# One stage for the first norm, the row projection and the query projection of a hybrid attention layer

## The reference

```
h = rmsnorm(x, norm1_g)                # x: 1024 prompt rows and 32 sample rows, 1024 wide
z = h @ w_in                           # 2848 columns
q_fox, k_fox, v_fox = 512 columns each       # 8 forgetting-attention heads of 64
f     = 8 columns -> logf = log_sigmoid(f + b_forget), later summed along the sequence
q_nsa = 512 columns                          # 8 sparse-attention heads
nsa   = 512 columns, win = 256 columns       # keys and values of the sparse attention and its window
gates = 24 columns -> sigmoid
```

## Time and profile before

| | |
|---|---|
| median of 3 runs | 2229.72 us (2228.98 to 2230.72) |
| profiled execution, its own time | 2237.79 us |
| span of the profiled execution | 2236.1 us |
| PE busy | 1909.3 us, 85% |
| DVE, ACT, POOL busy | 997.5, 723.5, 555.0 us |
| mean granted PE clock | 0.916 of full |

### The profile page before, as it was taken

The page is one execution under the profiler, slowest core; times in us unless marked ns, Lnnn a source line. Parts: engine busy times, 40 slices in busy tenths (PEclk is TensorE's granted clock), DMA queues, the critical chain, the costliest instruction groups (busy, mean ns, idle before and its releaser), DMA issues. The chain is left out here.

```text
span 2236.1 us, 32314 instructions
## 1 busy us (share of the span) xinstructions
PE 1909.3 (85%) x11816; PEld 1676.1 (75%) x11816; DVE 997.5 (45%) x1872; ACT 723.5 (32%) x1433; POOL 555.0 (25%) x644
## 2 busy tenths in 40 slices
PE   3996897996574738999999969899999999979996
PEld 2886796775552438788888858699999999966674
DVE  2323323112231324677777755433323333356897
ACT  2223112111221201777777753211211121133352
POOL 4310012124515132122222130111212222143452
PEclk9897898998786855999999989999999999989998
DMA  5532536322958283222222032211111111054533
GB/s 136 96 77 87 179 131 232 113 93 68 304 173 266 91 157 73 60 63 58 66 57 58 1 125 85 66 52 43 47 47 40 54 38 56 28 190 150 179 132 130
DMA packets 175169, 229.18 MB, mean 102 GB/s; under 512 B 44140, under 2 KB 120357, under 8 KB 174919
## 3 DMA queue, kind: packets, MB, share of 16 engines
q1 hardware_dynamic: 147930, 146.09, 21.8%
q0 software_dynamic: 27120, 81.55, 12.9%
HBM read 192.62 MB, written 40.18 MB: 104 GB/s over the span
## 5 line engine op out<-in xcount | busy, mean ns | idle before, releaser
L2290 DVE TENSOR_TENSOR pa_probs_T_lo<-pa_t,pa_probs_T_hi 128x512 fp32r<-128x512 f32 (+3 forms) x288 | 147.6, 533 | 64.5 <-ACT pa_probs_T_hi L2231 63.6
L121 PE MATMUL gate_acc<-o_T_hi,w_gate_split_hi 128*128 128x352 f32 x528 | 171.6, 325 | 2.0 <-ACTq L2669 2.0
L121 PE MATMUL up_acc<-o_T_hi,w_up_split_hi 128*128 128x352 f32 x528 | 170.4, 323 | 0.7 <-DVEq L2712 0.7
L122 PE MATMUL gate_acc<-o_T_lo,w_gate_split_hi 128*128 128x352 f32 x528 | 170.3, 323 | 0.0
L123 PE MATMUL gate_acc<-o_T_hi,w_gate_split_lo 128*128 128x352 f32 x528 | 170.2, 322 | 0.0
L122 PE MATMUL up_acc<-o_T_lo,w_up_split_hi 128*128 128x352 f32 x528 | 169.2, 321 | 0.0
L123 PE MATMUL up_acc<-o_T_hi,w_up_split_lo 128*128 128x352 f32 x528 | 169.1, 320 | 0.0
L2231 ACT ACTIVATE pa_probs_T_hi<-pa_t 128x512 fp32r<-128x512 f32 (+3 forms) x288 | 131.8, 472 | 91.3 <-PE pa_t L2156 88.0
L2156 PE MATMUL pa_t<-ident,pa_scores 128*128 128x128 f32 x816 | 138.9, 276 | 17.6 <-DVE pa_probs_T_lo L2290 17.6
L2216 ACT ACTIVATE pa_scores<-pa_scores,pa_neg_max 128x128 f32<-128x128 f32 (+1 forms) x192 | 143.3, 746 | 30.3 <-DVE pa_neg_max L2254 26.0
L121 PE MATMUL y_acc<-w_down_split_hi,act_split_hi 128*128 128x512 f32 x308 | 125.3, 407 | 18.9 <-DVE act_split_lo L3034 18.9
(11 more groups left out here) (444 smaller groups left out, 4773.5 us busy)
## 6 DMA issues: line engine op xcount, KB each, us to landing
w_down_raw<-in_w_down SPq DMA_DIRECT2D x59, 512.0 KB, 4.7
fox_k_pages<-in_cache_fox_kv SPq DMA_DIRECT2D x64, 256.0 KB, 8.3
w_rows<-in_cache_fox_kv POOLq DMA_DIRECT2D x64, 256.0 KB, 6.5
w_gate<-in_w_gu SPq DMA_DIRECT2D x22, 512.0 KB
w_up<-in_w_gu SPq DMA_DIRECT2D x22, 512.0 KB
sel_pages<-in_cache_nsa_kv POOLq DMA_DIRECT2D x64, 128.0 KB, 7.5
pa_k_fox<-scratch_kf_d POOLq DMA_DIRECT2D x32, 256.0 KB
w_rows<-in_w_in SPq DMA_DIRECT2D x3, 2048.0 KB, 14.5
```

The costliest lines, as they stand in the source:

```text
L121: pe.matmul(out, a[0][at], b[0][bt], start=start, stop=False)
L122: pe.matmul(out, a[0][at], b[1][bt], start=False, stop=False)
L2290: dve.tensor_tensor(lo, PT[n % 2][:, 0:m * P].rearrange("p (m n) -> p m n", n=P), hi, ALU.subtract).then_inc(s_cd, 1)
```

## The change

The three stages norm, queries and rows become one, `project`. Its steps are the 36 steps of the row stage, and behind them 24 query steps (chunks 4 and 5, q_fox and q_nsa with 512 columns each; twelve steps per chunk, 128 columns by a third of the rows). They use the same `z_acc`, `z` and `kt` buffers and the same weight buffers as the row steps.

- **Norm.** The tiles 0 and 1 are normalised and turned ahead of the first product. Tile t + 2 is normalised and turned around step t of the first chunk (k_fox): the steps need only their own tile of `hT`.
- **Loads.** The opening issues the loads of the first two tiles of `x` (once its tables are made) and of the k_fox weights (once its last page rows are turned). For this the weight buffers `w_rows`, the tiles of the norm and the second split weight buffer have fixed places at the far end of SBUF (`far_end`), and the opening's page rows and raw weights lie there too.
- **Log forget and gates.** The chain is spread over the query steps: ACT in steps 2 to 5 of the queries, DVE in 5, 6, 9 and 10, PE in 7, POOL's stores after 9 and 13. The sums are now kept in rows 64 to 71 of `c.cum`, which are zeroed again at the end.
- **Query results.** 128 x 352 per step: ACT copies with the scale, DVE splits into `kt`, POOL stores the pieces.

The core of the diff:

```diff
@@ front, SP @@
             load_rows(sp, mybir.EngineType.SP, 2, 0)
+            sp.wait_ge(s_pe, 4)
+            for t in range(2):
+                sp.dma_start(c.n1_x[t][:, :], d["x_prompt"][0, t * P:(t + 1) * P, :]).then_inc(c.s_x1[t], 16)
+            sp.wait_ge(s_tr, len(turns))
+            sp.dma_start(c.wr[0][:, :, :], d["w_in"][0].rearrange("(k p) n -> p k n", p=P)[:, :, C_KF:C_KF + 512]).then_inc(c.s_wr[0], 16)
...
+def project(c):
...
+    steps = [(ci, t) for ci in range(4) for t in range(NR)] + [(ci, x) for ci in (4, 5) for x in range(12)]
...
+            sp.dma_start(g[:, :], d["norm1_g"][0:1, :].to_broadcast([P, D])).then_inc(s_g, 16)
+            for t in range(2, 4):
+                sp.dma_start(x[t][:, :], d["x_prompt"][0, t * P:(t + 1) * P, :]).then_inc(c.s_x1[t], 16)
+            sp.dma_start(w[1][:, :, :], w_in[:, :, C_VF:C_VF + 512]).then_inc(s_w[1], 16)
+            for t in range(4, NR):
+                sp.wait_ge(s_xn, t - 3)
...
+            def product(s):
+                ci, t = steps[s]
                 if s >= 2:
                     pe.wait_ge(s_z, s - 1)
+                if ci == 0:
+                    pe.wait_ge(s_nl, t + 1)
...
+            turn_x(0)
+            turn_x(1)
+            n = 0
+            for s, (ci, t) in enumerate(steps):
+                product(s)
+                if ci == 0 and t + 2 < NR:
+                    turn_x(t + 2)
                 if n < len(tsteps) and tsteps[n] < s:
                     transposes(n)
                     n += 1
...
+            squares(0)
+            root(0)
+            rounded(0, [0])
+            squares(1)
+            root(1)
+            rounded(0, [1])
+            copy(0)
+            rounded(0, [2, 3])
+            copy(1)
+            for s, (ci, t) in enumerate(steps):
+                if ci == 0 and t + 2 < NR:
+                    squares(t + 2)
+                    root(t + 2)
+                if ci and t == 1 and ci + 1 < len(chunks):
+                    rounded(ci + 1, range(PIECES))
+                evacuated(s)
+                if ci == 0 and t + 2 < NR:
+                    copy(t + 2)
+                if ci == 0 and t + 2 == NR - 1:
+                    rounded(1, range(PIECES))
...
+            scale(0)
+            rests(0, [0])
+            scale(1)
+            rests(0, [1])
+            rest(0)
+            rests(0, [2, 3])
+            rest(1)
...
             for s, (ci, t) in enumerate(steps):
+                if ci == 0 and t + 2 < NR:
+                    scale(t + 2)
+                if n < len(ksteps) and ksteps[n] < s:
+                    key_copies(n)
+                    n += 1
+                if ci == 0 and t + 2 < NR:
+                    rest(t + 2)
+                if ci == 0 and t + 2 == NR - 1:
+                    rests(1, range(PIECES))
```

More of the change, by code:

```diff
@@ L276, in front @@
         w1 = split(ph, "cmp_w1_split", [P, 2, 16, 256])
-        raw = [ph.sb(f"cmp_w1_raw{i}", [P, 8, 256]) for i in range(2)]
+        rows = [ph.far(f"cmp_rows{i}", [P, 4, 4, 2, HD]) for i in range(SB)]
+        raw = [ph.far(f"cmp_w1_raw{i}", [P, 8, 256]) for i in range(2)]
         w2 = c.w2
@@ L808, in project_rows @@
     }
-    steps = [(ci, t) for ci in range(4) for t in range(9)]
+    steps = [(ci, t) for ci in range(4) for t in range(NR)] + [(ci, x) for ci in (4, 5) for x in range(12)]
+    rowwise = [ci < 4 for ci, t in steps]
+    NROW = sum(rowwise)
+    FIRST_Q = NROW
     KP = 2
@@ L839, in project_rows @@
         tp = [ph.ps(f"z_tp{i}", [P, 4, P]) for i in range(2)]
-        lp = [ph.ps(f"lf_tp{i}", [P, 4, P]) for i in range(3)]
+        ntp = [ph.ps(f"n1_tp{i}", [P, KD, P]) for i in range(2)]
+        lp = [ntp[0][:, 0:4, :], ntp[0][:, 4:8, :], ntp[1][:, 0:4, :]]
+        s_g = ph.sem("n1_gain_loaded")
+        s_ss, s_ms, s_rt, s_rr, s_xn = (ph.sem(f"n1_{n}") for n in ("squares", "mean", "root", "inverse", "normed"))
+        s_nt, s_nh, s_nl = (ph.sem(f"n1_{n}") for n in ("turned", "copied", "rest_kept"))
         s_hi = ph.sem("w_rows_rounded")
@@ L880, in _, with turn_x @@
         def _(pe):
+            def turn_x(t):
+                rows = ROWS[t]
+                pe.wait_ge(s_xn, t + 1)
+                if t >= 2:
+                    pe.wait_ge(s_nl, t - 1)
+                for k in range(KD):
+                    ins = pe.transpose(ntp[t % 2][:, k, 0:rows], xn[t % 2][0:rows, k * P:(k + 1) * P], c.ident[0:rows, 0:rows])
+                ins.then_inc(s_nt, 1)
             def transposes(n):
@@ L930, in _, with evacuated @@
-            rounded(0)
-            for s, (ci, t) in enumerate(steps):
-                rows = ROWS[t]
-                if t == 1 and ci + 1 < len(chunks):
-                    rounded(ci + 1)
+                    act.wait_ge(s_acc, sum(1 for a, t in steps if a < ci - 1))
+                for k in pieces:
+                    at = np.s_[:, k * KP:(k + 1) * KP, 0:width(ci)]
+                    act.activation(ws[ci % 2][0][at], w[ci % 2][at], ACT.Copy).then_inc(s_hi, 1)
+            def evacuated(s):
+                ci, t = steps[s]
@@ L954, in stores_before, with scale @@
         def stores_before(n):
[L955 removed]
+            return sum(1 for m in range(n) if m % 2 == n % 2 and kept(m))
         @block.vector
         def _(dve):
+            def scale(t):
+                rows = ROWS[t]
+                dve.wait_ge(s_ss, t + 1)
+                dve.tensor_scalar(ms[0:rows, t:t + 1], ss[0:rows, t:t + 1], 1.0 / D, EPS, ALU.mult, ALU.add).then_inc(s_ms, 1)
+                dve.wait_ge(s_rt, t + 1)
+                dve.reciprocal(rr[0:rows, t:t + 1], rt[0:rows, t:t + 1]).then_inc(s_rr, 1)
+                dve.wait_ge(s_rr, t + 1)
+                if t == 0:
+                    dve.wait_ge(s_g, 16)
+                if t >= 2:
+                    dve.wait_ge(s_nt, t - 1)
+                dve.scalar_tensor_tensor(out=xn[t % 2][0:rows, :], in0=x[t % 4][0:rows, :], scalar=rr[0:rows, t:t + 1],
+                                         in1=g[0:rows, :], op0=ALU.mult, op1=ALU.mult).then_inc(s_xn, 1)
@@ L1074, in _ @@
-            pool.wait_ge(s_fo, 48)
+                pool.wait_ge(s_ks[i], 32 * sum(1 for m in range(len(ksteps)) if m % 2 == i and kept(m)))
+            pool.wait_ge(s_fo, 32)
 def misc(c, name, rows, a=None, b=None):
```

485 lines of the change are left out of this document (182 added, 303 removed).

## The result

The changed kernel takes 2199.64 us in the median of 4 runs (2195.29 to 2203.48), the kernel before 2229.35 in the same session; the ratio is 0.986, interval 0.985 to 0.987. It is faster, by 1.4%, which is 30 us and not the 49.8 forecast: 2199.64 lies outside the range of 2172 to 2192. Its profiled execution took 2202.11 us (span 2200.4), 35.7 less than the one of before. All but 0.3 of that lies ahead of the sample attention, whose first product moved from 554.88 to 519.44 us (-35.4) where 505.1 was forecast; the rest of the program took 1681.0 us after and 1681.2 before. So 14.3 us are missing in the profiled pair. The other 6 between the pair and the medians have no row: before's profiled execution stood 8.4 us over its median, after's 2.5.

The account below looks back on a forecast made before the run. The stretch was taken as bound by PE while multiplying, otherwise by chains of small steps, loads and barriers. Gains of 56.2 us less costs of 6.4 gave 49.8, so 2180 us from a median of 2229.72; range 2172 to 2192.

Parts of the forecast that it names:

- When the first product can start: Opening and first norm tiles: the first product moves from 239.7 to 208.0 us, a gain of 31.7.
- One restart instead of two: Start of products: one of two restarts at half clock goes, saving 2.5 us; the other stays.
- What is added on PE: First chunk and queries: seven turns of x between key products cost 5.6 us, nine log-forget transposes 0.8.
- The clock rival: First ten steps: transposes keep PE at 1.2 GHz, +57 us, ending at 2237; chance 0.02.
- The log transposes: Nine small transposes of log forget, moved into the query steps, cost PE 0.8 us.
- query steps: Query chunks: each step of 24 products takes 3.82 us, with shape, operands and clock as before.
- What must hide beside key products: First chunk: norm, key splits and loads hide beside products of 6.8 us steps; cost 0, cover 0.9 us.
- The rival of the store ring: Query steps: late stores returning kt buffers set the pace, +15 us to 2195, or 2186 if only the end; chance 0.09.
- The prediction's list of what would show it wrong: Signs: query steps over 3.9 us, PE waiting for xn or hT in each tile, or clock near 0.5.
- The new end: Last product to next stage: 10.9 us instead of 18.4, modelled on the old query stage's end; gain 7.5.
- The norm chain: First chunk: rival that the norm shows by 1 to 2 us at each of seven tiles, 2187 to 2194; chance 0.08.
- The opening's loads: Opening: x and weights landed by about 192 us; rival that they are late, +6 to 2186, within a 0.05 chance.

Follow-up runs that it names:

- e1: The changed kernel with the 4 MB window copy and its wait left out: 2188.5 us.
- e3: The changed kernel with the whole window copy issued in the v chunk, behind the win weights load: 2187.02 us.
- e5: e3 with the 60 query stores issued by SyncE with their own semaphores instead of by POOL: 2180.10 us.
- e6: e3 with the first two x tiles and first weights loaded at the stage's start instead of in the opening: 2195.49 us.

## Why the prediction was wrong, step by step

**When the first product can start: right, in part by luck**, 207.52 for 208.0, but two errors met. The chain to the reciprocal was done at 199.36 and not at 200.6 (its squares began at 196.50, not 197.05), and the gain was 1.60 us late behind it where 0.5 stood, so that the scaling began at 200.96 for 201.1:

```profile
200.96 1.28 DVE L881 SCALAR_TENSOR_TENSOR n_xn<-n_x,n_rr,n_gain 128x1024 f32<-128x1024 f32 x1 [1.60 <-DMA n_gain<-in_norm_g]
```

**One restart instead of two: right**, and the one left was short, 2.6 us at clock 0.52 (5.3 to 5.5 in the earlier trace rows): 1.3 us to the good. The stall brought a second one behind it (clock 0.54 from 258.00 to 261.50), which is counted in the stall.

**What is added on PE: right for the turns.** The five full steps take 6.88 to 6.89, for 6.8, in the runs without a stall. The clock rival fell. From 210.10 to 246.00 the clock was 1.00, PE busy all the time, with eight turns behind each step and four key transposes from the second on. The sentence of the Trainium skill (TensorE: Matmul & The Clock Gate, Part 4: PE-mode transpose), that full clock does not engage for transposes, doesn't carry over to these transposes between products. By the rival that was built on it a step would have taken over 10.3 us (24 products at 0.43). The log transposes cost 1.2 us and not 0.8, and from there on query steps took 3.88 to 3.89 instead of 3.82, another 1.1 us in all, in every kernel here; its cause is open.

**What must hide beside key products: the step that failed.** "The SyncE queue moves the 4 MB window copy behind the last x load, with the nsa weights behind it; these are used only after nine steps" looked at who needs the data, and put the price at 0. What counted was who shares the DMA engines with it. The key stores did, the kt ring covers a landing of 8.8 us, and the copy made it 21.9. e1 and e3 put the price at 10.7 to 11.4 us of stage, against 11.3 read from the steps.

Before, the copy stood in the same chunk, and no engine waited for a key store. The rows show when it was issued and when the stores were:

```profile
346.65 0.85 SPq L863 DMA_DIRECT2D out_win_kv_s<-in_state_win_kv  x1
```

```profile
L1043 POOL DMA_DIRECT2D scratch_kf_d<-kt_hi x8: 750/751/782, 364.9 to 406.9; - x8
```

```profile
DMA to landing us min/median/max: 2.8/3.8/9.0
```

The first key store came 18 us behind the copy's issue, and the copy's packets ran from 348.2 to 370.1, so it met only their end; now the stores of the second key tile stand 4 us behind it. The z store issued at 358.09, in the copy's middle, did take 12.8 us to land, and its ring of three covered that. So the change moved the copy on top of the key stores, and it also queued the norm behind the key split. Whether such a late store would have held PE in the old lists was not tested. The rival of the store ring was the right mechanism in the wrong place: it was tried on the queries alone, with a landing of 5.0 from the earlier trace rows. There the split stores landed in 7.0 us at most and held VectorE twice, for 5.6 and 3.9 us, and PE never. The row that told of the copy, the 12.8 us of that z store, was not among those read. The prediction's list of what would show it wrong did name a wait of PE for xn.

**The new end: a term mis-sized**, 14.0 for 10.9. It was modelled on the old query stage's end, with 20 POOL DMAs, and a drain of 1.70 us in it. Here it is 7.17. e5 shows it: 5.1 without it.

The sum of what the profiled execution lost against the forecast: 11.3 (stall) + 3.1 (end) + 1.1 (query steps) + 0.4 (log transposes) - 1.3 (restart) - 0.5 (start) = 14.1 of the 14.3 us.

**The other rivals.** The norm chain did show only when VectorE was held up; alone it stayed hidden (e1). The opening's loads were there: DVE and ACT waited for no weights before the first product, and e6 puts their worth at 8 to 9 us.

## What to carry to other kernels

When a transfer has no reader nearby, ask who else is on the DMA engines while it runs, and which ring then waits. Compare the longest landing with what the ring covers, not the median; and look at the transfer's shape, since 2 MB in one transfer with four packets at a time held up a store for as long as 4 MB did, and 2 MB in four transfers did not. An engine's in-order list passes a wait on to all that stands behind it, so a stage that merges two lists merges their waits as well. When a stage is merged, look again at what each background transfer now runs beside. At a block's end, look at which sequencer reaches the barrier last and why, and give its last work to a queue that ends sooner.

## What the runs showed of the hardware that was not expected

A store's landing went from 2.8 us to 21.9 beside one transfer over eight sequences, to 21.5 beside one of half its bytes, and to 8.7 beside those bytes in four transfers. POOL's drain at the end of a block took 7.169 us in all ten profiled executions of kernels with the same POOL stores, to the nanosecond, though all of its transfers had landed, 6.189 with 12 of them less and 2.94 with 60 less. With the same loop and operands a 352-column product came every 0.159 us at first and every 0.162 from the log transposes on, at a granted clock of 1.00 in both (440 to 462 us and 462 to 505); the cause is open.
